# The last expert block's rows stay on chip: a 0/1 matrix product in place of the last trip through HBM

## The reference

```python
for e in range(N_EXPERTS):                       # 16 experts
    gu = t @ w_in[e]                             # 1024 -> 768
    act = jax.nn.silu(gu[:, :D_EXPERT]) * gu[:, D_EXPERT:]
    y = y + gates[:, e:e + 1] * (act @ w_out[e]) # 384 -> 1024
```

## Time and profile before

| | us |
|---|---|
| three timed executions, median | 1541.89 |
| span of the profiled execution, first to last instruction (the profile gives no other time of it) | 1538.2 |
| TensorE busy | 1429.7 (93% of the span) |
| VectorE busy | 986.0 (64%) |
| ScalarE busy | 776.9 (51%) |
| GpSimd busy | 144.7 (9%) |
| mean granted TensorE clock | 0.968 of full speed |

### The profile page before, as it was taken

The page is one execution under the profiler, slowest core; times in us unless marked ns, Lnnn a source line. Parts: engine busy times, 40 slices in busy tenths (PEclk is TensorE's granted clock), DMA queues, the critical chain, the costliest instruction groups (busy, mean ns, idle before and its releaser), DMA issues. The chain is left out here.

```text
span 1538.2 us, 19917 instructions
## 1 busy us (share of the span) xinstructions
PE 1429.7 (93%) x7821; PEld 1207.6 (79%) x7821; DVE 986.0 (64%) x1311; ACT 776.9 (51%) x1138; POOL 144.7 (9%) x160
## 2 busy tenths in 40 slices
PE   8999899999999996999995999999999997999993
PEld 6887677887888686999984888887888686999982
DVE  4574658686465457999975423563356457999973
ACT  4422655485344445777753325323145445777750
POOL 1000011200000002222210000000000002221210
PEclk9999899989999997999997999999999998999997
DMA  6713111133521075999984423223330076999965
GB/s 208 140 48 112 59 55 56 46 120 110 209 83 55 0 282 229 380 364 376 382 302 188 125 89 101 84 83 123 115 104 32 6 284 237 386 367 365 386 237 208
DMA packets 110865, 274.48 MB, mean 178 GB/s; under 512 B 41762, under 2 KB 44211, under 8 KB 106164
## 3 DMA queue, kind: packets, MB, share of 16 engines
q1 hardware_dynamic: 95506, 203.96, 38.0%
q10 hardware_dynamic: 5762, 52.44, 8.5%
q0 software_dynamic: 9504, 16.80, 3.0%
HBM read 265.75 MB, written 25.17 MB: 189 GB/s over the span
## 5 line engine op out<-in xcount | busy, mean ns | idle before, releaser
L185 DVE TENSOR_TENSOR w_lo<-w_stage,w_hi 128x2048 fp32r<-128x2048 f32 (+2 forms) x32 | 67.1, 2103 | 164.9 <-ACT w_hi L175 155.1
L175 ACT ACTIVATE w_hi<-w_stage 128x2048 fp32r<-128x2048 f32 (+2 forms) x34 | 60.2, 1773 | 213.1 <-PE bank L244 109.9
L200 DVE TENSOR_TENSOR w_lo<-w_stage,w_hi 128x2048 fp32r<-128x2048 f32 x42 | 96.1, 2289 | 47.2 <-ACT w_hi L194 22.1
L194 ACT ACTIVATE w_hi<-w_stage 128x2048 fp32r<-128x2048 f32 x40 | 76.6, 1915 | 83.4 <-PE bank L244 48.2
L3051 PE MATMUL bank<-e_wi_lo,e_hx_hi 128*128 128x384 f32 x256 | 86.4, 338 | 0.0
L3050 PE MATMUL bank<-e_wi_lo,e_hx_hi 128*128 128x384 f32 x256 | 86.4, 337 | 0.0
L2903 DVE TENSOR_TENSOR e_wi_lo<-e_room,w_hi 128x1536 fp32r<-128x1536 f32 x40 | 68.6, 1751 | 11.8 <-ACT w_hi L2899 11.7
L2907 POOL DMA_INDIRECT e_tok<-moe_h,moe_slots x32 | 65.6, 2050 | 83.3 <-DVE moe_slots L2609 57.4
L2903 DVE TENSOR_TENSOR e_wi_lo<-e_room,w_lo 128x1536 fp32r<-128x1536 f32 x40 | 70.0, 1750 | 1.8 <-ACT w_lo L2899 1.6
L2899 ACT ACTIVATE w_hi<-e_room 128x1536 fp32r<-128x1536 f32 x40 | 57.6, 1495 | 18.1 <-PE bank L244 18.1
L2899 ACT ACTIVATE w_lo<-e_room 128x1536 fp32r<-128x1536 f32 x40 | 59.4, 1486 | 5.2 <-PE bank L3051 5.2
(11 more groups left out here) (562 smaller groups left out, 3862.7 us busy)
## 6 DMA issues: line engine op xcount, KB each, us to landing
e_room<-in_moe_w_in SPq DMA_DIRECT2D x88, 768.0 KB, 10.4
w_stage<-in_moe_w_in SPq DMA_DIRECT2D x40, 768.0 KB, 11.0
e_wo<-in_moe_w_out ACTq DMA_DIRECT2D x16, 1536.0 KB, 10.4
e_room<-in_moe_w_out ACTq DMA_DIRECT2D x14, 1536.0 KB, 10.9
w_stage<-in_x_wkv SPq DMA_DIRECT2D x16, 1024.0 KB, 5.1
w_stage<-in_sg_w_in SPq DMA_DIRECT2D x16, 1024.0 KB, 5.4
w_stage<-in_hyb_w_in SPq DMA_DIRECT2D x10, 1024.0 KB, 5.2
w_stage<-in_x_wq SPq DMA_DIRECT2D x8, 1024.0 KB, 5.0
```

The costliest lines, as they stand in the source:

```text
L175: act.activation(self.w_hi[h][:, :, :cols], self.stage[h][:, :, :cols], ACT.Copy)\
L185: dve.tensor_tensor(self.w_lo[h][:, :, :cols], self.stage[h][:, :, :cols], self.w_hi[h][:, :, :cols], ALU.subtract).then_inc(self.lo_done[ ...
L194: act.activation(self.w_hi[h][:, :, :cols], self.stage[h][:, :, :cols], ACT.Copy).then_inc(self.hi_done[h], 1)
L200: engine.tensor_tensor(self.w_lo[h][:, :, :cols], self.stage[h][:, :, :cols], self.w_hi[h][:, :, :cols], ALU.subtract).then_inc(self.lo_do ...
```

## The change

The last block's rows (those of the loop's last turn) are no longer scattered. They stay in PSUM, are split into `y_hi` (ScalarE) and `y_lo` (VectorE) in the room of `wo_hi` and `wo_lo`, and the next phase multiplies them by a 0/1 matrix `spot` [128 block rows, 512 tokens], which has a one where a block row belongs to a token: `spread`, two matmuls of 128x512 for each tile of tokens and half of the features. The result is in PSUM, one row for each token, and `add` brings it into x with the token's weight `m.sel` (zero where the token has no row in that block). `last_weights` makes `m.sel` after block 10; the loop makes `spot`, in each turn.

All other rows are read back earlier: after block 14's scatter has landed and the loop's weights are split (`settled`), SP issues all eight reads, in the order (3, 0), (0, 0), (0, 1), (3, 1), then tiles 1 and 2. Tile 0's are added by VectorE and tile 3's by ScalarE (scaling) and GpSimd (adding) still within the expert block; tile 1's by VectorE and tile 2's by ScalarE and GpSimd in the next phase. Rows of `moe_y` that are no longer written must hold zeros: cross-attention now fills `moe_y` with zeros (one memset on GpSimd, eight writes of 128 rows on SP, and a wait for them on SP).

In the loop VectorE now copies block 14's half out after two of the four splits.

```diff
@@ Combine
-    ORDER = [c * T + i for i in range(T) for c in range(2)]
+    ORDER = [(3, 0), (0, 0), (0, 1), (3, 1), (1, 0), (1, 1), (2, 0), (2, 1)]
+    BANKS = ((0, 1), (2, 3), (5, 7), (6, 7))
-    def load(self, engine, part):
-        for j in self.ORDER[part::2]:
+    def load(self, engine):
+        for t, c in self.ORDER:
+            j = c * T + t
...
+    def add_stored(self, dve, t, c, summed, n):
...
         dve.scalar_tensor_tensor(out=m.x[:, t, :], in0=self.y[:, j, :], scalar=m.wgt[:, j:j + 1],
-                                 in1=m.x[:, t, :], op0=ALU.mult, op1=ALU.add).then_inc(self.added, 1)
+                                 in1=m.x[:, t, :], op0=ALU.mult, op1=ALU.add).then_inc(summed, 1)
+    def scale_stored(self, act, t, scaled):
+        for c in range(2):
+            j = c * T + t
+            act.wait_ge(m.y_in[j], 16 * (self.layer + 1))
+            act.activation(self.y[:, j, :], self.y[:, j, :], ACT.Copy, scale=m.wgt[:, j:j + 1]).then_inc(scaled, 1)
+    def add_scaled(self, pool, t, scaled, summed):
+        for c in range(2):
+            pool.wait_ge(scaled, c + 1)
+            if c:
+                pool.wait_ge(summed, 1)
+            pool.tensor_tensor(m.x[:, t, :], m.x[:, t, :], self.y[:, c * T + t, :], ALU.add).then_inc(summed, 1)
+    def spread(self, pe, t, n):
+        for term, part in enumerate(self.y_parts):
+            ins = pe.matmul(self.bank(t, n)[:, :], self.spot[:, t * P:(t + 1) * P], part[:, n * GC:(n + 1) * GC],
+                            start=term == 0, stop=term == 1)
+        ins.then_inc(self.spread_out, 1)
+    def spread_first(self, pe):
+        for t in range(T):
+            for n in range(2 if t < T - 1 else 1):
+                self.spread(pe, t, n)
+    def spread_rest(self, pe):
+        pe.wait_ge(self.added, self.ready(T - 2))
+        self.spread(pe, T - 1, 1)
+    def add(self, dve, t):
+        if t == 1:
+            dve.wait_ge(self.stored_1, 2)
+        if t == 2:
+            dve.wait_ge(self.stored_2, 2)
+        for n in range(2):
+            cols = slice(n * GC, (n + 1) * GC)
+            dve.wait_ge(self.spread_out, 2 * t + n + 1)
+            dve.scalar_tensor_tensor(out=m.x[:, t, cols], in0=self.bank(t, n)[:, :], scalar=m.sel[:, t:t + 1],
+                                     in1=m.x[:, t, cols], op0=ALU.mult, op1=ALU.add).then_inc(self.added, 1)
@@ store_x (VectorE; TensorE, ScalarE and GpSimd get blocks of their own)
+            combine.spread_first(pe); combine.spread_rest(pe)
+            combine.scale_stored(act, 2, combine.scaled_2)
+            combine.add_scaled(pool, 2, combine.scaled_2, combine.stored_2)
+            combine.add_stored(dve, 1, 0, combine.stored_1, 0)
+            combine.add(dve, 0)
+            combine.add_stored(dve, 1, 1, combine.stored_1, 1)
+            for t in range(1, T):
+                combine.add(dve, t)
@@ cross_attend
+                pool.memset(zero[:, :], 0.0).then_inc(zero_made, 1)
+                for j in range(2 * T):
+                    sp.dma_start(y_dram[j * P:(j + 1) * P, :], zero[:, :]).then_inc(y_cleared, 16)
+                sp.wait_ge(y_cleared, 16 * 2 * T)
@@ sgu_layer
+                    combine.add_scaled(pool, 2, combine.scaled_2, combine.stored_2)   # GpSimd, first
+                        if h == 0 and b == 1:
+                            combine.spread_rest(pe)
+                        if h == 0 and b > 1:
+                            pe.wait_ge(combine.added, combine.ready(T - 1) - (3 - b))
+                    combine.spread_first(pe)                                          # ahead of turn(0)
+                    combine.scale_stored(act, 2, combine.scaled_2)                    # ahead of square(0)
+                    combine.add_stored(dve, 1, 0, combine.stored_1, 0)
+                    combine.add(dve, 0)
+                    combine.add_stored(dve, 1, 1, combine.stored_1, 1)
                     for i in range(T):
                         nt.normalize(dve, i)
                         if i + 1 < T:
-                            combine.add(dve, i + 1, 1)
-                        if i + 2 < T:
-                            combine.add(dve, i + 2, 0)
+                            combine.add(dve, i + 1)
@@ moe_experts
-                sp.wait_ge(stored[1], 16 * (NE // 2))
-                combine.load(sp, 0)
+                sp.wait_ge(settled, 1)
+                combine.load(sp)
...
-                scatter(None, 1, ix[:, 1:2])
-                pool.wait_ge(stored[1], 16 * (NE // 2))
+                pool.wait_ge(stored[1], 16 * (NE // 2 - 1))
+                for q in range(CI):
+                    pool.wait_ge(w.wi_los[q], n + L)
+                pool.sem_inc(settled, 1)
+                combine.add_scaled(pool, T - 1, scaled, summed_late)
...
                     m.split_hi(act, upcoming)
+                combine.scale_stored(act, T - 1, scaled)
                 act.wait_ge(wo_used, n + L)
-                act.wait_ge(stored[1], 16 * (NE // 2 - 1))
-                finish(1)
-                act.wait_ge(stored[1], 16 * (NE // 2))
-                combine.load(act, 1)
+                for g in range(2):
+                    act.activation(y_hi[:, g * GC:(g + 1) * GC], y_ps[g][:, :], ACT.Copy).then_inc(last_hi, 1)
...
+                def last_weights():      # six small instructions on VectorE, after block 10
...
-                    dve.wait_ge(wo_used, i + L)
-                    dve.wait_ge(stored[0], i * 16 + 16 * (NE // 2 - 1))
-                    finish(0)
+                        if q == 1:
+                            dve.wait_ge(wo_used, i + L)
+                            dve.wait_ge(stored[0], i * 16 + 16 * (NE // 2 - 1))
+                            finish(0)
+                    dve.tensor_copy(last_row[:, :], slots[:, 1, bass.ds(i + L, 1)]).then_inc(spotted, 1)
...
+                    for t in range(T):
+                        ins = dve.tensor_scalar(spot[:, t * P:(t + 1) * P], rt.p_row[:, :], spots[:, t:t + 1], None, ALU.is_equal)
...
                 n = rest(dve)
+                for c in range(2):
+                    combine.add_stored(dve, 0, c, summed, c)
                 if upcoming is not None:
                     m.split_lo(dve, upcoming)
-                dve.wait_ge(wo_used, n + L)
-                dve.wait_ge(stored[1], 16 * (NE // 2 - 1))
-                finish(1)
+                for g in range(2):
+                    dve.wait_ge(last_hi, g + 1)
+                    dve.tensor_tensor(y_lo[:, g * GC:(g + 1) * GC], y_ps[g][:, :], y_hi[:, g * GC:(g + 1) * GC], ALU.subtract).then_inc(last_lo, 1)
```

More of the change, by code:

```diff
@@ L1740, in wait @@
         engine.wait_ge(self.added, self.ready(t))
[L1742 to L1747, removed]
-                                 in1=m.x[:, t, :], op0=ALU.mult, op1=ALU.add).then_inc(self.added, 1)
+    def add(self, dve, t):
+        m = self.m
+        if t == 1:
[7 more added lines that the diff above has]
+                                     in1=m.x[:, t, cols], op0=ALU.mult, op1=ALU.add).then_inc(self.added, 1)
 class Arrival:
@@ L2138, in cross_attend, with _ @@
         sums = m.sb(t, f"{name}_sums", [P, NU, 2])
+        zero = m.sb(t, f"{name}_zero", [P, D])
+        zero_made, y_cleared = m.psem(f"{name}_zero_made"), m.psem(f"{name}_y_cleared")
         v = memory.v
         with nc.Block() as block:
+            @block.gpsimd
+            def _(pool):
+                pool.memset(zero[:, :], 0.0).then_inc(zero_made, 1)
+            @block.sync
+            def _(sp):
+                sp.wait_ge(zero_made, 1)
+                for j in range(2 * T):
+                    sp.dma_start(y_dram[j * P:(j + 1) * P, :], zero[:, :]).then_inc(y_cleared, 16)
+                sp.wait_ge(y_cleared, 16 * 2 * T)
             @block.tensor
@@ L2347, in rest @@
                         pe.wait_ge(lo_out, 2 * b + h + 1)
+                    combine.spread_first(pe)
                     turn(0)
@@ L2941, in moe_experts @@
         be, ebf = tile("be", [1, OV, NE]), tile("ebf", [1, OV + 2])
+        tile_row = tile("tile_row", [P, T])
         wi_used = [m.psem(f"{nm}_wi_used{q}") for q in range(CI)]
         made, ov_c, placed, ov_out, listed = (m.psem(f"{nm}_{s}") for s in ("made", "ov_c", "placed", "ov_out", "listed"))
+        settled, spotted, summed, scaled, summed_late, last_hi, last_lo = (
+            m.psem(f"{nm}_{s}") for s in ("settled", "spotted", "summed", "scaled", "summed_late", "last_hi", "last_lo"))
+        here, alone, last_row, side, spots = tile("here", [P, 2 * T]), tile("alone", [P, 1]), tile("last_row", [P, 1]), tile("side", [P, 1]), tile("spots", [P, T])
+        y_hi, y_lo, spot = wo_hi[:, 0, :], wo_lo[:, 0, :], wo_hi[:, 1, 0:S]
+        combine.hold_last(y_hi, y_lo, spot)
         stored = [m.sem(f"{nm}_stored{j}") for j in range(2)]
@@ L3398, in build_trunk @@
         right = [ExitStack() for layer in range(DEPTH)]
+        y_dram = [nc.dram_tensor(f"moe{layer}_y", [2 * S, D], F32).ap() for layer in range(DEPTH)]
```

(2 more changed lines are left out.)

63 lines of the change are left out of this document (43 added, 20 removed).

## The result

The changed kernel takes 1552.48 us (median of four runs, 1549.83 to 1555.24) against 1542.76 for the kernel before on the same chip. The ratio is 1.0067, with a 95% interval of 1.005 to 1.0083. Forecast was 1534.2, a gain of 7.7; the change lost about 10. Its profiled execution has a span of 1548.1 us, 9.9 more than before.

What follows compares the result with a forecast made beforehand. Bound: the moe_y round trip and adds at the kernel's end and after layer 0, TensorE between. Gains of 6.9 and 1.6 less a loss of 0.8 in the expert blocks took 1541.89 to 1534.2 us; range 1529 to 1542.

Steps and rivals of the forecast that it cites:

- `last_weights`: After block 10: six chained small VectorE instructions lengthen TensorE's next block by 0.4 us a layer, a loss of 0.8.
- the zeroing: In cross-attention: filling moe_y with zeros takes some 13 us of DMA while the engines are idle, costing nothing.
- rival 4: Both boundaries: GpSimd's adds become the bound; gain gone from 3.7 us each, 1546.6 us at 4.5; chance 0.08.
- The choice that GpSimd gives way: After layer 0: a running GpSimd add yields to VectorE, norm ends near 840.3; gain of 1.6, otherwise loss of 1.5.
- Rival 1: After layer 0: GpSimd holds VectorE out for its whole instruction, a loss of 1.5; total 1537.3 us; chance 0.20.
- The reads: Both last expert blocks: the eight moe_y reads start at 815.3 and 1503.8, once block 14's scatter, issued earlier, has landed.
- rival 3: Both layers: reads land 3 us late through shared DMA traffic and scaling ahead of the last copy; 1540.2 us; chance 0.15.
- Its second mechanism: Last expert block: scaling of tile 3 stands ahead of the last product's copy on ScalarE; forecast had it just fit.
- The phase change after GpSimd: Kernel's end: GpSimd ends the last expert block at 1516.2 and the last phase begins 1.0 us later, at 1517.2.
- the 1.75 us to come back: Layer 1's first turn: spreads keep TensorE busy, so full clock returns by then and product 0 ends 27.0 after, not 28.75.

Runs made afterwards that it cites:

- e4: Changed kernel with m.sel put in the unused part of k_eps's 32 bytes, so every tile keeps its old address; 1544.51 us, ratio 1.0006.
- e2: Kernel before plus only an unused tile of 16 bytes a partition, allocated where the change allocates m.sel; 1552.93 us, ratio 1.0066.
- v4: The second version with the last block's output weights loaded only after block 14's scatter landed, and a fourth stored piece added before y_lo; 1536.4 us, ratio 0.996.
- the second version: Changed kernel with all stored adds on VectorE, m.sel in k_eps's room, each tile's second piece added after the previous tile's normalization; 1528.11 us, ratio 0.9904.

## Why the prediction was wrong

**The step that failed** is the sum's silence about everything between the two boundaries: "Between these two places TensorE is the bound, and only what delays it counts there." The only terms taken for it were `last_weights` and the zeroing. The added tile `m.sel` was read as arithmetic and never as 32 bytes that move its neighbours. It costs 9.4 us here (`e4`), 10.2 alone (`e2`): more than the whole forecast gain, and the sign of the result. None of the rivals held it, rival 4 least of all, whose slower case came from another mechanism.

With the addresses restored, the change stands at +1 us where -7.7 was forecast. Those 8.7 are in these steps:

- **The choice that GpSimd gives way: wrong, 3.1 us by its own sum.** Rival 1 described what happened. The row at 15.00 in the earlier trace rows, which decided it, was of another kind (a tensor_scalar with one input) and half the size; why the two ran side by side there is not shown. The Trainium skill's rule ("SBUF — State Buffer", section "SBUF: two separate sides": the first to come has the port pair for its whole instruction) agrees with every stretched row above (3.11, 3.22, 3.17 us for 1.28) to within 0.2 us, and the rows at 828.17 and 233.59 are the same rule the other way round. The turn came at 844.9 when the lag of 1.34 that TensorE brought along is taken off 846.24; the forecast was 840.3, rival 1 had 843.4.
- **The reads: 2.1 us late at the end, 2.7 after layer 0.** With the lag taken off they were issued at 1520.21 - 14.33 = 1505.88 and at 819.32 - 1.34 = 817.98; forecast were 1503.8 and 815.3. Block 14's scatter was issued as much earlier as forecast, but landed only behind the 1.5 MB of weights (`v4`), and the loop's end added about 1 us. That is rival 3's traffic. (The 396 GB/s of the earlier trace rows were not SP's alone, as the prediction reads them: of 2.38 MB in that stretch SP's queue moved 1.81. Alone, it moved 413 GB/s in the kernel after, from 1526 to 1530, so the sum loses nothing by it.) Its second mechanism was there too: the scaling at 1528.46 held `y_hi` back by 1.8 us, hidden behind GpSimd.
- **The phase change after GpSimd: 2.9 us, forecast 1.0.** The 1.0 was counted from the last read's issue (831.81 in the kernel before). But there too GpSimd closed the block last: its DRAIN of 2.69 us began at 829.89, when the last scatter had landed, and ended at 832.58, 0.24 before ScalarE's 832.82. So the price was in the trace of before, under the reads. At the end of the kernel this is 1.9 us; after layer 0 VectorE ended the block, at 836.55, and it cost nothing.
- **The clock: the 1.75 us to come back did not.** The spreads were to bring TensorE to the turn at full clock. They ran at half (0.50) until they were nearly through, and after 3.40 us of standing TensorE made the turn at half again:

```profile
836.80:842.00 5.20, 5.13 (x12) 4.10 (x13) 4.83 (x4) 4.90 (x7) 2.50 (x3) 0.50 0.61 106
843.00:846.20 3.20, 0.00 (x0) 0.00 (x0) 3.18 (x2) 0.00 (x0) 3.20 (x2) 0.93 1.01 240
846.20:851.00 4.80, 3.98 (x13) 3.22 (x14) 2.83 (x6) 2.41 (x5) 1.09 (x2) 0.50 1.01 381
```

(Stretches of the kernel after: us, busy us of PE, PEld, DVE, ACT, POOL, granted clock, DMA share, GB/s.) In the second version, where TensorE stood 1.71 us between spreads and turn, the turn took 1.09 and not 1.97.

Together: at 850.77 the lag had grown by 6.86 - 1.34 = 5.5 where 1.6 were to be gained, 7.1 off, and the end gained 4.4 for 6.9, 2.5 off. These 9.6 come from one trace and the 8.7 from medians, and they agree within what medians can tell.

**What was right.** GpSimd's add of 128x1024 takes 2.35 alone (2.43 forecast), so rival 4's condition (3.7) was not met. The zeroing was free: HBM writes rose from 25.17 to 32.51 MB and no lag stands there. `last_weights` made the two blocks behind it 13.96 and 13.85 us long in place of 13.76 and 13.77, 0.3 a layer against 0.4. The end of the kernel was faster for the reason given.

## What to carry to other kernels

Before counting instructions, ask what a new tile moves: compare the start addresses of the operands of the large products, and put small tiles where they move nothing. Don't give GpSimd an elementwise SBUF operation beside two-input work of VectorE on the path: it takes 2.35 us where VectorE takes 1.28, and VectorE stands for all of it. Look at each engine's DRAIN before moving the end of a block onto it: GpSimd took 2.6 us to close the expert block whatever it had done last, which is free only while another engine ends at least that much later.

## What the runs showed of the hardware

- The start address of a tile in SBUF sets the pace of 128x512 fp32r matmuls: on average 227 ns from start to start with both operands at a multiple of 128 bytes; 233 with one of them 32 bytes below such a multiple, whichever operand it is; at 64 past a multiple of 128, 229 for the stationary and 233 for the moving operand. No other addresses were tried.
- GpSimd's DRAIN at the end of the expert block ends 2.61 to 2.69 us after its last instruction or wait, behind an add of 8 columns as of 1024 and behind none. Where it ends last, the next phase begins 2.90 us after GpSimd's add; 0.33 after VectorE's last instruction where that ends last (0.63 in the row at 837.17). In the last phase of the kernel after, GpSimd's DRAIN ended 0.08 us after its add.
- An indirect scatter of 0.5 MB issued beside a 1.5 MB load on another queue landed after 5.5 us, and after 3.3 with that load held back.
